# First two weight tiles of a three-block layer kernel worked by pairs of row blocks

## The chip, the cores and the metric

One core of one Trainium2 chip runs the whole program. The metric is the device time of one execution in microseconds (us); lower is better. Times inside an execution are us from the start of its span.

## The reference, cut to what matters

Three blocks run one after the other on x of 512 rows and 2048 columns, all in float32. The part that the change touches is the head of block 1:

```
h = x * rsqrt(mean(x*x, axis=-1) + 1e-6) * norm_pre      # rows of x, 512 x 2048
proj = h @ w_in                                          # 2048 x 5120 weights
u_s, g_s, q_d, k_d, v_d, g_d, q_x, g_x = split(proj)     # u_s: the first 1024 columns
```

u_s goes into a state-space scan, the others into two kinds of attention and gates; a memory of 256 rows is normalised and projected too. The mixed result is multiplied by w_out, normalised and added to x. Blocks 2 and 3 have the same outline (norm, projection, mixing, output projection) with other mixers.

## The kernel before, in words

**Precision.** A float32 product is made of three passes over rounded parts: a value is split into an upper part (`hi`, rounded to fp32r) and a lower part (`lo`, the rest). For a weight slice and the activations h the kernel adds hi x hi, hi x lo(h) and lo x hi(h).

**Weights.** A weight tile is 128 columns wide and 2048 deep. It comes in two slices of 128 x 1024 (8 steps k of 128 each) through a ring of four slots. SP issues the loads in order (L3198); the load of a slot's next slice waits until TensorE has used the old one: `part_used` for the first slice of a tile, the bank's full semaphore for the last. ScalarE makes the upper part (L3350, `split`), VectorE the lower (L3392).

**Head of block 1.** Rows are taken in four blocks of 128 (`tt` 0 to 3). For each: `x_rstd` makes the sum of squares (blocks 0 and 3 on ScalarE, L723; blocks 1 and 2 on VectorE, L885), the mean (VectorE, L887), the root (ScalarE, L725), the reciprocal and a diagonal matrix of it (VectorE, L889, L891). `x_turn` multiplies the rows by that diagonal on TensorE (L506), which turns and scales them at once: four quarters of a PSUM bank, eight matmul records each. `x_parts` takes the bank into the upper part of h on ScalarE (L745, sixteen instructions, four a bank) and the lower part on VectorE (L911, sixteen), which then frees the bank. The lower part overlies the rows of x in SBUF.

**Banks.** `x_turn` and the small transposes `ss_0` (L529, for the state matrix) take their banks in turn from the five side banks 3 to 7, and each take waits until the bank's former user is released (`bk.take`). Tiles take theirs from banks 0 to 2.

**Tiles.** A tile in mode "T" keeps the weights stationary and moves the 512 rows: 16 steps k, three passes each, 48 matmuls of 512 columns into one bank (L3265). Tile 0 (`ut[0]`) waits at every fourth k for the release of all four row blocks' quarter (`first_tile_waits`). Then ScalarE copies the bank to `us` (L694) and GpSimd stores it (L430).

**Order.** One list, `script`, sets the order of the work on every engine: each engine walks it and does its own share of each step. In it stand, for the head, x_rstd 0, x_turn 0, x_rstd 1, x_turn 1, x_parts 0, x_rstd 2, x_turn 2, x_rstd 3, x_turn 3, b1_tables (GpSimd loads, after the fourth turn), x_parts 1 to 3, ss_0, then tile 0, ss_1, tile 1, ss_2, the norms of the memory (m_rstd), tile 2, m_turn 0, ss_3, tile 3, m_turn 1, powers, tile 4. The split steps are put in by a loop (L3087 on): a slice's step goes in ahead of a `target` step. In the kernel before, tile 0's first slice is split ahead of x_parts 3, and its second and both of tile 1 ahead of tile 0, behind ss_0. Tile 2's are split ahead of tile 1, that is behind ScalarE's copy of tile 0.

The matmuls of block 2 at L3275 are of another mode ("N"): h is stationary and a weight slice 256 columns wide moves. They are named here since the prediction reads their rows.

Of the kernel before, what the change touches and what calls it, by code (L numbers as in the profile page):

```python
# [13 lines left out]
P = 128  # L14
# [3 lines left out]
TT = SEQ // P  # L18
# [4 lines left out]
SLOT = 1024  # L23
# [107 lines left out]
def block1(K):  # L131
    nc, T, ps, bk = K.nc, K.T, K.ps, K.bk
# [49 lines left out]
    t = K.arena(0, Bf)  # L182
# [5 lines left out]
    t = K.arena(0, Bf)  # L188
# [8 lines left out]
    w = K.arena(vst_at)  # L197
# [4 lines left out]
    w = K.arena(rope_at)  # L202
    ang, kk_ = w("ang", SEQ), w("turns", SEQ)
    w = K.arena(rope_at)
    scan_1, scan_2 = w("scan_1", 2, 8, S_G // 2), w("scan_2", 2, 8, S_G // 2)
    w = K.arena()
# [7 lines left out]
    w = K.arena()  # L214
# [12 lines left out]
    def tile(name, i):  # L227
# [7 lines left out]
        else:  # L235
# [1 line left out]
        return st  # L237


    script = [("x_rstd", 0), ("x_turn", 0), ("x_rstd", 1), ("x_turn", 1), ("x_parts", 0), ("x_rstd", 2), ("x_turn", 2),  # L240
              ("x_rstd", 3), ("x_turn", 3), ("b1_tables", 0), ("x_parts", 1), ("x_parts", 2), ("x_parts", 3), ("ss_0", 0)]
    ut = [tile("us", i) for i in range(S_C)]
    mt = [t_ for h in range(XA_H) for t_ in (tile("mk", h), tile("mv", h))]
# [5 lines left out]
    glu = [tile("glu", i) for i in range(8)]  # L249
# [41 lines left out]
    n = 0  # L291
# [225 lines left out]
        pe.wait_ge(s_diag, TT + tt + 1)  # L517
        turn_rows(pe, st, mem_rows[:, tt, :], diag[:, tt, :])

    def first_tile_waits(pe, kk):  # L520
        if kk % 4 == 0:
            for tt in range(TT):
                pe.wait_ge(*bk.released(("x_turn", tt), kk // 4))

    def pe_ss_0(pe, st):
# [752 lines left out]

    def glu_waits(pe, kk):
        pe.wait_ge(s_clo, kk + 1)  # L1280
    K.tiles[ut[0]]["by_k"], K.tiles[glu[0]]["by_k"] = first_tile_waits, glu_waits
    K.stage("pool", b1_tables=pool_tables, tile1=pool_tile, sp_a=pool_sp_a, sp_b=pool_sp_b,
            scan=pool_scan, sp_d=pool_sp_d, y_back=pool_y_back, wo1=pool_wo)
    K.stage("pe", x_turn=pe_x_turn, m_turn=pe_m_turn, ss_0=pe_ss_0, sp_a=pe_sp_a, sp_b=pe_sp_b, sp_c=pe_sp_c, sp_d=pe_sp_d,
# [1579 lines left out]
class Kit:  # L2864


    def __init__(self, nc, ctx, T):
        self.nc, self.ctx, self.T = nc, ctx, T
        self.at = {"pe": {}, "act": {}, "vec": {}, "pool": {}}
        self.uses, self.tiles, self.params = {}, {}, {}  # L2870
        self.norm_gain, self.par_count, self.wo_src = {}, {}, {}
        self.y_base, self.y_count = {}, 0
        self.slot_src, self.slot_count, self.slot_used = {}, {"wo": 8}, {}
        self.const_loads, self.wait_gain, self.par_at = [], {}, 0
        self.sp_start, self.mix_parts, self.norm_parts, self.norm_gain_wait = [], {}, {}, {}
        self.sq_junk, self.wo_releases = {}, {}
        self.wo_mids, self.mids, self.wo_order, self.mix_wait, self.mix_src = {}, {}, {}, {}, {}

    def keep(self, *dims):
# [34 lines left out]
    def tile(self, st, srcs, mode, w, act, n, kt=KT, bias=None, after=(), releases=1, lo=None,  # L2914
             lo_from=0, full=None):


        self.tiles[st] = dict(srcs=srcs, mode=mode, w=w, act=act, n=n, kt=kt, bias=bias, after=list(after),
                              releases=releases, lo=lo, per=SLOT // max(w, P), lo_from=lo_from, full=full, pool="P", by_k=None)

    def rounded(self, name, *dims):

# [9 lines left out]
def build(nc, T, out, blocks):  # L2932
    with ExitStack() as ctx:
        K = Kit(nc, ctx, T)
# [10 lines left out]
        ring, ring_lo = K.rounded("ring", RING, SLOT)  # L2945
        ring_hi = K.sb("ring_hi", RING, SLOT, dt=F32R)
# [13 lines left out]
        full = [K.sem(f"bank{i}_full") for i in range(8)]  # L2960
# [3 lines left out]
        part_used = K.sem("part_of_stage_used")  # L2964
        s_hi, s_lo = K.sem("weight_upper_ready"), K.sem("weight_lower_ready")
# [70 lines left out]
        script = []  # L3036
# [10 lines left out]
        for blk in blocks:  # L3047
# [3 lines left out]
            if blk in K.norm_parts:  # L3051
                for tt in range(TT):
                    after = script.index(("norm", blk, min(tt + 1, TT - 1)))
# [17 lines left out]
        def slot_subs(st):  # L3071
            return K.tiles[st]["kt"] // K.tiles[st]["per"] if st[0] == "tile" else K.slot_count.get(st[0], 0)
# [10 lines left out]
        for n, st in enumerate(script):  # L3083
            subs = slot_subs(st)
            for sub in range(subs):
                slots.append((st, sub))
                stage_at[st] = n  # L3087
                if is_split(st, sub):
                    target = st if sub >= 2 or len(slots) == 2 else earlier if subs == 1 else before
                    assert len(slots) <= RING or stage_at[slots[-1 - RING][0]] <= stage_at[target]  # L3090
                    ahead.setdefault(target, []).append(("split", st, sub))
            if subs:
                before, earlier = st, before
# [14 lines left out]
        script = [s_ for st in script for s_ in order(st)]  # L3108
        split_no = {st[1:]: n for n, st in enumerate([st for st in script if st[0] == "split"])}

        for st in script:
# [3 lines left out]
            elif st[0] == "tile":  # L3115
                t = K.tiles[st]
# [12 lines left out]
        slot_of, slot_value, slot_view, count, loads = {}, {}, {}, [0] * RING, []  # L3129
        parts = 0  # L3130
        for n, (st, sub) in enumerate(slots):
            i = n % RING
            if st[0] == "tile":
                t = K.tiles[st]
# [8 lines left out]
                subs = slot_subs(st)  # L3143
            elif st[0] in K.slot_src:
                view = lambda r, i=i: r[:, i, :]
                dmas = K.slot_src[st[0]](st, sub, ring[:, i, :])
                last, subs = K.slot_used[st[0]](st, sub), 1
            else:
                w = K.wo_src[st[1]][0]
# [3 lines left out]
                last, subs = bk.filled(st, 3), 8  # L3153
# [21 lines left out]
        def columns(ap, kk, tt=None):  # L3175
# [4 lines left out]
                return ap[:, :, kk, :] if tt is None else ap[:, tt, kk, :]  # L3180
            return ap[:, kk, :] if tt is None else ap[:, kk, tt * P:(tt + 1) * P]

        block = ctx.enter_context(nc.Block())

        @block.sync
# [33 lines left out]
        def _(pe):  # L3219
            pe.wait_ge(K.s_const, const_total)  # L3220
            pe.wait_ge(s_made, 2)
            for st in script:
                if st in inner:
                    continue
                if st[0] == "norm":
                    pe.wait_ge(s_hn, hn_at[st] + 1)
                    for k4 in range(KT // 4):
                        bk.take(pe, st, k4)
# [220 lines left out]
```

## Time and profile before

| | |
|---|---|
| median of 3 runs | 3064.72 us |
| lowest, highest | 3061.41, 3065.34 us |
| profiled execution | 3060.2 us |
| its span | 3058.4 us |
| TensorE matmul busy | 2925.0 us, 96% |
| VectorE, ScalarE, GpSimd busy | 46%, 35%, 10% |
| mean granted clock of TensorE | 0.969 |

The profiled execution is one run of its own; its span is from the first to the last instruction, and its own time has 1.8 us around that. In the rows further down PE is TensorE, PEld its weight loads, DVE VectorE, ACT ScalarE, POOL GpSimd and SPq the queue of SP, which issues DMAs. Busy shares are means over the whole program and tell nothing of a single stage.

### The profile page before, as it was taken

The page shows a single profiled execution, that of the slowest core. Times are in us where ns is not written, and L with a number is a line of the kernel's source. Part 1 is how long each engine was busy: PE and PEld are TensorE (multiplying, and loading weights), DVE is VectorE, ACT ScalarE, POOL GpSimd, SP SyncE. Part 2 cuts the span into 40 slices and gives each one's busy share as a digit, 9 for nine tenths or more (in the row PEclk, how much of TensorE's full clock was granted, in tenths as well). Part 3 has the DMA queues.
Part 4 walks back from the last instruction along what each step waited for, and adds up shares of the span by engine and source line. Part 5 has one row for each costly group of instructions (what it writes and reads, how often), then busy time and mean ns, then how long its engine had stood idle before and what let it go on. Part 6 is the DMA issues. An engine that isn't in the chain of part 4 may idle for free.

```text
span 3058.4 us, 36911 instructions
## 1 busy us (share of the span) xinstructions
PE 2925.0 (96%) x14916; PEld 2366.6 (77%) x14916; DVE 1414.3 (46%) x2435; ACT 1057.2 (35%) x1740; POOL 302.3 (10%) x530
## 2 busy tenths in 40 slices
PE   7999999999988999999999977999999999999997
PEld 6788878888866888888887865777777776777786
DVE  5566634445234545545544234135444543443533
ACT  5223233453235333222223245235444542222321
POOL 5346044100000000000000000000000000000000
PEclk9999999999998999999999988999999999999999
DMA  7466455324334544465664332332222222222332
GB/s 187 113 173 126 105 118 124 101 83 166 97 109 131 151 145 131 145 186 173 189 181 159 97 116 62 82 91 69 72 67 70 69 76 69 62 62 76 128 98 105
DMA packets 440136, 349.05 MB, mean 114 GB/s; under 512 B 72352, under 2 KB 389984, under 8 KB 435744
## 3 DMA queue, kind: packets, MB, share of 16 engines
q1 hardware_dynamic: 406544, 241.86, 28.6%
q0 software_dynamic: 33424, 104.84, 11.9%
q8 instruction: 119, 1.95, 0.3%
q14 instruction: 49, 0.40, 0.0%
HBM read 322.78 MB, written 22.81 MB: 113 GB/s over the span
## 4 chain that ended last, share of the span: by engine, by line
PE 91%; DVE 4%; ACT 3%; issue 1%; DMA 0%; DVEq 0%; SPq 0%; ACTq 0%
PE bank L3265 56%; PE bank L3301 17%; PE bank L3275 3%; PE bank L2183 1%; PE bank L2234 1%; PE bank L2210 1%; PE bank L2255 1%; PE bank L589 1%; PE bank L584 1%; PE bank L2294 1%; PE bank L653 1%; PE bank L2152 1%; PE bank L506 1%; PE bank L2312 1%; PE bank L554 0%
## 5 line engine op out<-in xcount | busy, mean ns | idle before, releaser
L3392 DVE TENSOR_TENSOR ring_parts<-ring,ring_hi 128x1024 fp32r<-128x1024 f32 (+1 forms) x420 | 505.5, 1217 | 805.9 <-ACT ring_hi L3350 801.7
L3265 PE MATMUL bank<-A_parts,ring_hi 128*128 128x512 f32 (+1 forms) x1616 | 655.5, 406 | 24.8 <-DVE ring_parts L3392 17.8
L3350 ACT ACTIVATE ring_hi<-ring 128x1024 fp32r<-128x1024 f32 (+1 forms) x420 | 437.2, 1053 | 658.6 <-DMA ring<-in_w_in 347.3
L3265 PE MATMUL bank<-A_parts,ring_parts 128*128 128x512 f32 (+1 forms) x1616 | 637.1, 394 | 0.0
L3265 PE MATMUL bank<-X_parts,ring_hi 128*128 128x512 f32 (+1 forms) x1424 | 557.6, 392 | 0.0
L3265 PE MATMUL bank<-B_parts,ring_hi 128*128 128x512 f32 (+1 forms) x1272 | 503.9, 396 | 4.5 <-DVE X_parts L3380 4.5
L3265 PEld LDWEIGHTS bank<-A_parts,ring_hi 128*128 128x128 f32 (+1 forms) x1616 | 307.3, 190 | 100.6 <-issue 30.2
L3265 PEld LDWEIGHTS bank<-A_parts,ring_parts 128*128 128x128 f32 (+1 forms) x1616 | 306.7, 190 | 70.9 <-issue 0.6
L3265 PEld LDWEIGHTS bank<-X_parts,ring_hi 128*128 128x128 f32 (+1 forms) x1424 | 267.8, 188 | 57.3 <-issue 2.0
L3265 PE MATMUL bank<-B_parts,ring_parts 128*128 128x512 f32 (+1 forms) x784 | 305.8, 390 | 0.0
L3301 PE MATMUL bank<-ring_hi,A_parts 128*128 128x512 f32 x768 | 301.1, 392 | 1.6 <-issue 0.9
L3301 PE MATMUL bank<-ring_hi,B_parts 128*128 128x512 f32 x768 | 300.7, 392 | 1.8 <-DVE A_parts L3399 1.8
L3265 PEld LDWEIGHTS bank<-B_parts,ring_hi 128*128 128x128 f32 (+1 forms) x1272 | 239.9, 189 | 61.1 <-issue 6.3
L3265 PE MATMUL bank<-work_parts,ring_hi 128*128 128x512 f32 (+1 forms) x616 | 231.1, 392 | 0.0
L3301 PE MATMUL bank<-ring_parts,A_parts 128*128 128x512 f32 x512 | 199.9, 390 | 0.0
L3301 PEld LDWEIGHTS bank<-ring_hi,A_parts 128*128 128x128 f32 x768 | 145.3, 189 | 33.3 <-issue 3.1
L3265 PEld LDWEIGHTS bank<-B_parts,ring_parts 128*128 128x128 f32 (+1 forms) x784 | 145.8, 186 | 32.6 <-issue 0.7
L3301 PEld LDWEIGHTS bank<-ring_hi,B_parts 128*128 128x128 f32 x768 | 145.3, 189 | 32.3 <-issue 1.8
L3265 PEld LDWEIGHTS bank<-work_parts,ring_hi 128*128 128x128 f32 (+1 forms) x616 | 115.0, 187 | 24.5
L1764 DVE SCALAR_TENSOR_TENSOR work<-work,par 128x1024 f32<-128x1024 f32 x90 | 115.5, 1283 | 3.0
L2438 ACT ACTIVATE work<-work 128x128 f32<-128x128 f32 (+3 forms) x128 | 70.5, 553 | 132.3 <-DVE work L2598 132.3
L1744 POOL DMA_DIRECT2D work<-in_w_ada x96 | 50.7, 528 | 639.6 <-DVE work L1764 519.6
(507 smaller groups left out, 3322.6 us busy)
## 6 DMA issues: line engine op xcount, KB each, us to landing
ring<-in_w_in SPq DMA_DIRECT2D x288, 512.0 KB, 3.8
ring<-in_w_out SPq DMA_DIRECT2D x96, 512.0 KB, 3.7
work<-in_w_ada POOLq DMA_DIRECT2D x96, 512.0 KB, 4.7
ring<-in_w_in SPq DMA_DIRECT2D x48, 256.0 KB, 3.7
ring<-in_w_mem_kv SPq DMA_DIRECT2D x16, 512.0 KB, 4.2
x_keep<-X POOLq DMA_DIRECT2D x8, 1024.0 KB, 4.7
X<-x_keep POOLq DMA_DIRECT2D x8, 1024.0 KB, 10.2
X<-in_x SPq DMA_DIRECT2D x4, 1024.0 KB, 10.6
```

The source lines that it names most:

```text
L506: mm = nc.tensor.matmul(ps(st, k4)[:, j * P:(j + 1) * P], lhsT=rows[:, kk * P:(kk + 1) * P], rhs=scale, start=True, stop=True)
L584: nc.tensor.matmul(cols[r], lhsT=T2[c % 2][:, g * P:(g + 1) * P], rhs=U2[c % 2][:, g * S_B:(g + 1) * S_B], start=True, stop=False)
L589: mm = nc.tensor.matmul(cols[r][:, 1:S_B], lhsT=C2[c % 2][rows, s, q, :], rhs=vst[rows, s, 0:S_B - 1, 4 * c + q], start=False, stop=(s == 1))
L653: mm = nc.tensor.matmul(ps(st)[:, 0:P], lhsT=pT[:, u % 2, kt * P:(kt + 1) * P], rhs=rhs, start=(kt == 0), stop=(kt == n - 1))
L1744: pool.dma_start(slots[:, n % ADA_SLOTS, :], T["w_ada_3"][0][kp * P:(kp + 1) * P, part * ADA_W:(part + 1) * ADA_W]).then_inc(s_load[n % AD ...
L1764: ins = nc.vector.scalar_tensor_tensor(acc[:, :], w, sc[:, kp:kp + 1], acc[:, :], ALU.mult, ALU.add)
L2438: nc.scalar.activation(e, e, ACT.Exp, bias=mx[:, n % 2, i:i + 1], scale=-1.0, accum_out=sums[:, n % 2, i:i + 1]).then_inc(s_exp, 1)
L3265: mm = nc.tensor.matmul(K.ps(st)[0:w, 0:t["n"]], lhsT=wp[:, j, :], rhs=columns(ap, kk), start=first, stop=end)
L3275: mm = nc.tensor.matmul(o, lhsT=columns(ap, kk, tt), rhs=wp[:, j, :], start=first and opens and t["bias"] is None, stop=end, skip_group_ch ...
L3301: mm = nc.tensor.matmul(K.ps(st, tt), lhsT=y[:, kk, rows], rhs=w[:, j, :], start=(no == 0 and m == 0), stop=(no == KT - 1 and m == 2), ski ...
L3350: nc.scalar.activation(slot_view[key](ring_hi), slot_view[key](ring), ACT.Copy).then_inc(s_hi, 1)
L3392: nc.vector.tensor_tensor(slot_view[key](ring_lo), slot_view[key](ring), slot_view[key](ring_hi), ALU.subtract).then_inc(s_lo, 1)
```

## The change

The change does three things. The sum of squares of row block 2 (`x_rstd` 2) moves ahead of `x_parts` 0 in the script. The four split steps of tiles 0 and 1 all move ahead of `x_parts` 2. And TensorE works tiles 0 and 1 together in two passes (`tiles_by_pair`): for row blocks 0 and 1 both tiles with all their k, then for row blocks 2 and 3 both tiles again, out of the same slices, which stay in the ring. Each matmul then moves 256 columns. The waits for the parts of h are for the pair's two row blocks alone. A slot is given back in the second pass.

```diff
-    script = [("x_rstd", 0), ("x_turn", 0), ("x_rstd", 1), ("x_turn", 1), ("x_parts", 0), ("x_rstd", 2), ("x_turn", 2),
+    script = [("x_rstd", 0), ("x_turn", 0), ("x_rstd", 1), ("x_turn", 1), ("x_rstd", 2), ("x_parts", 0), ("x_turn", 2),
               ("x_rstd", 3), ("x_turn", 3), ("b1_tables", 0), ("x_parts", 1), ("x_parts", 2), ("x_parts", 3), ("ss_0", 0)]
...
-    def first_tile_waits(pe, kk):
+    def first_tile_waits(pe, kk, pair):
         if kk % 4 == 0:
-            for tt in range(TT):
+            for tt in (2 * pair, 2 * pair + 1):
                 pe.wait_ge(*bk.released(("x_turn", tt), kk // 4))
...
-    K.tiles[ut[0]]["by_k"], K.tiles[glu[0]]["by_k"] = first_tile_waits, glu_waits
+    K.tiles[ut[0]]["by_pair"], K.tiles[glu[0]]["by_k"] = first_tile_waits, glu_waits
+    K.paired_tiles[1] = ut[0:2]
+    for st in ut[0:2]:
+        for sub in range(2):
+            K.split_at[st, sub] = ("x_parts", 2)
...
                     target = st if sub >= 2 or len(slots) == 2 else earlier if subs == 1 else before
+                    target = K.split_at.get((st, sub), target)
...
+        def row_pair(ap, kk, pair):
+
+            if isinstance(ap, tuple):
+                ap, kk = ap[kk // 8], kk % 8
+            if len(ap.shape) == 4:
+                return ap[:, 2 * pair:2 * pair + 2, kk, :]
+            return ap[:, kk, 2 * pair * P:2 * (pair + 1) * P]
...
+            def tiles_by_pair(sts):
+
+                for pair in range(2):
+                    for st in sts:
+                        t = K.tiles[st]
...
+                        if pair == 0:
+                            bk.take(pe, st)
+                        subs, w, per = slot_subs(st), t["w"], t["per"]
+                        o = K.ps(st)[0:w, 2 * pair * P:2 * (pair + 1) * P]
+                        for sub in range(subs):
+                            pe.wait_ge(s_lo, split_no[st, sub] + 1)
+                            hi, lo = slot_view[st, sub](ring_hi), slot_view[st, sub](ring_lo)
+                            for j in range(per):
+                                kk = sub * per + j
+                                if t["by_pair"]:
+                                    t["by_pair"](pe, kk, pair)
+                                for n, (wp, ap) in enumerate(((hi, t["act"]), (hi, t["lo"]), (lo, t["act"]))):
+                                    mm = nc.tensor.matmul(o, lhsT=wp[:, j, :], rhs=row_pair(ap, kk, pair),
+                                                          start=pair == 0 and kk == 0 and n == 0,
+                                                          stop=pair == 1 and kk == t["kt"] - 1 and n == 2, skip_group_check=True)
+                            if pair == 1 and sub < subs - 1:
+                                mm.then_inc(part_used, 1)
+                        if pair == 1:
+                            mm.then_inc(bk.full_sem(st, 0), 1)
+
             for st in script:
                 if st in inner:
                     continue
-                if st[0] == "norm":
+                if st in in_pairs:
+                    if st in [sts[0] for sts in K.paired_tiles.values()]:
+                        tiles_by_pair(K.paired_tiles[st[1]])
+                elif st[0] == "norm":
```

## Rows read from the trace of the kernel before

**Rows 1.** The page: the chain that ended last, by line, share of the span.

```profile
PE bank L3265 56%; PE bank L3301 17%; PE bank L3275 3%; PE bank L2183 1%; PE bank L2234 1%; PE bank L2210 1%; PE bank L2255 1%; PE bank L589 1%; PE bank L584 1%; PE bank L2294 1%; PE bank L653 1%; PE bank L2152 1%; PE bank L506 1%; PE bank L2312 1%; PE bank L554 0%
```

**Rows 2.** The chain within the first 60 us: start, length, piece.

```profile
27.47 5.50 PE bank L506 x24
...
35.30 1.13 DVE ring_parts L3392
36.43 1.05 DVE X_parts L911 x4
...
37.61 22.51 PE bank L3265 x98
```

**Rows 3.** Timeline of VectorE, 0 to 60: start, length, instruction, count, [idle before].

```profile
14.65 0.29 DVE L891 TENSOR_SCALAR work<-ident,rstd 128x128 f32<-128x128 f32 x1
...
20.20 2.28 DVE L885 CUSTOM_DVE_ANT_0 work<-X 128x2048 f32<-128x2048 f32 x1
...
26.29 7.33 DVE L911 SCALAR_TENSOR_TENSOR X_parts<-bank,par,A_parts 128x128 fp32r<-128x128 f32 x28 [0.55 <-ACT A_parts L745]
...
41.77 3.50 DVE L3392 TENSOR_TENSOR ring_parts<-ring,ring_hi 128x1024 fp32r<-128x1024 f32 x3 [1.21 <-ACT ring_hi L3350]
```

**Rows 4.** Waits of TensorE, 60 to 300: us in total, times, longest.

```profile
PE bank L3265 <- DVE ring_parts L3392: 4.0, 1, 4.0
```

**Rows 5.** The chain behind the second turn of memory rows.

```profile
88.63 0.69 DVE B L921
...
103.49 23.66 PE bank L3265 x96
```

**Rows 6.** The loads of x (L3190): issues, and time to landing.

```profile
L3190 SPq DMA_DIRECT2D X<-in_x x4: 416/428/655, 1.2 to 2.6; - x4
...
DMA to landing us min/median/max: 5.2/10.6/16.7
```

**Rows 7.** Timeline of ScalarE, 0 to 60.

```profile
14.33 1.13 ACT L745 ACTIVATE A_parts<-bank,par 128x128 fp32r<-128x128 f32 x4
...
22.82 1.89 ACT L723 ACTIVATE work<-X 128x2048 f32<-128x2048 f32 x1
...
25.13 7.34 ACT L745 ACTIVATE A_parts<-bank,par 128x128 fp32r<-128x128 f32 x28
...
40.70 2.94 ACT L3350 ACTIVATE ring_hi<-ring 128x1024 fp32r<-128x1024 f32 x3
```

**Rows 8.** Timeline of SP's queue, 0 to 60: loads of slices, then of memory rows.

```profile
3.30 18.85 SPq L3198 DMA_DIRECT2D ring<-in_w_in  x4
22.19 2.48 SPq L375 DMA_DIRECT2D B<-in_mem  x2
```

**Rows 9.** Stretches: busy and count of PE, PEld, DVE, ACT, POOL; clock, DMA, GB/s.

```profile
21.30:26.00 4.70, 1.16 (x8) 0.97 (x8) 2.39 (x8) 3.07 (x8) 0.00 (x0) 1.00 1.19 295
26.00:33.00 7.00, 5.53 (x26) 5.53 (x27) 6.71 (x26) 6.47 (x26) 0.00 (x0) 0.51 0.87 331
33.00:36.60 3.60, 3.60 (x33) 3.48 (x33) 3.06 (x9) 3.60 (x12) 0.00 (x0) 1.00 0.00 0
```

**Rows 10.** Timeline of TensorE: the small transposes ahead of tile 0.

```profile
36.50 0.33 PE L529 MATMUL bank<-ident,work 64*128 64x64 f32 x2
```

**Rows 11.** Two pieces of the whole chain; weight loads in the stretch of the second.

```profile
221.58 10.93 PE bank L3265 x48
...
980.98 22.81 PE bank L3275 x190
...
L3275 PEld LDWEIGHTS bank<-ring_hi,X_parts 128*128 128x128 f32 x64 | 8.8, 192 | 0.0
```

**Rows 12.** The slice loads (L3198) issued from 40 to 56.

```profile
DMA to landing us min/median/max: 3.9/4.2/4.7
```

**Rows 13.** Timeline of GpSimd, 35 to 60: its stores of tile 0.

```profile
51.99 4.25 POOL L430 DMA_DIRECT2D u_blocks<-work  x8
```

**Rows 14.** The core's span and mean granted clock.

```profile
core 0: 3058.4 us, clock 0.969
```

More of the change, by code:

```diff
@@ L2876, in __init__ @@
         self.sq_junk, self.wo_releases = {}, {}
+        self.split_at, self.paired_tiles = {}, {}
         self.wo_mids, self.mids, self.wo_order, self.mix_wait, self.mix_src = {}, {}, {}, {}, {}
@@ L2918, in tile @@
         self.tiles[st] = dict(srcs=srcs, mode=mode, w=w, act=act, n=n, kt=kt, bias=bias, after=list(after),
-                              releases=releases, lo=lo, per=SLOT // max(w, P), lo_from=lo_from, full=full, pool="P", by_k=None)
+                              releases=releases, lo=lo, per=SLOT // max(w, P), lo_from=lo_from, full=full, pool="P", by_k=None, by_pair=None)
     def rounded(self, name, *dims):
@@ L3221, in _ @@
             pe.wait_ge(s_made, 2)
+            in_pairs = {st for sts in K.paired_tiles.values() for st in sts}
+            def tiles_by_pair(sts):
+                for pair in range(2):
+                    for st in sts:
+                        t = K.tiles[st]
+                        assert t["mode"] == "T" and t["bias"] is None and st not in K.mids and not t.get("wait")
+                        for dep in t["after"]:
+                            if dep[0][2] // 2 == pair:
+                                pe.wait_ge(*bk.released(*dep))
+                        if pair == 0:
[17 more added lines that the diff above has]
+                            mm.then_inc(bk.full_sem(st, 0), 1)
             for st in script:
```

## The prediction, made before the changed kernel was run

> **What bounds the kernel now.** I read the chain of waits first: every line of any size in it is TensorE's, and the first, the split matmuls of the weight tiles (L3265), holds 56% [rows 1]. The kernel as a whole is bound by TensorE, so a change pays only if it takes TensorE's waits away or shortens its work. The change touches the first 60 us, so next I read the same chain there. It starts the weight tiles at 37.61 and from there runs 22.51 us through 98 matmuls with no other piece: tiles 0 and 1 are worked without a hole [rows 2]. Ahead of 37.61 the chain lies on VectorE and ScalarE: they make the parts of h out of the turned rows. VectorE ends row block 2 at 35.3, makes one weight slice (35.30, 1.13 of it on the chain), and ends the first quarter of row block 3 at 37.5, which releases TensorE [rows 2, 3]. So the first tile waits only for a quarter of row block 3, not for all of it: the change has little to win there.
>
> What follows the first tiles matters too. From 59.5 TensorE goes on through turns and tiles until a wait of 4.0 us before 103.49, and what it then waits for (the powers of the state matrix on VectorE) starts only when TensorE has ended its second turn of memory rows, at 88.6 [rows 4, 5]. A time won or lost by 59.5 is therefore carried on one for one; that wait absorbs nothing.
>
> **Squares of row block 2 forward.** VectorE is free at 14.94 and takes the square (2.28 us) there instead of at 20.20 [rows 3]. The four issues of x land 5.2 to 16.7 us after issue, median 10.6, the last issued at 2.6 [rows 6]; spread evenly, block 2 is there at about 14.6 (an estimate), so no wait. But the step moves on ScalarE as well: its root stands now ahead of row block 0's parts, which started at 14.33 [rows 7] and now start only behind the root. From the square's start (20.20) to ScalarE's first work behind the root (22.82) it was 2.6 us; so 14.94 + 2.6 = 17.6, 3.3 us later. ScalarE makes a part in 7.34/28 = 0.262 us, VectorE in 7.33/28 = 0.262, a block of 16 in 4.2 [rows 3, 7]. ScalarE ends block 0 at 21.8, squares block 3 and takes its root (22.82 to 25.13, 2.3 us): block 1's parts start at 24.1 on ScalarE, and 1.15 later, at 25.3, on VectorE, where they started at 26.29. **Gain 1.0 us.** VectorE ends block 1 at 29.5. TensorE's second turn is later than before (its banks are released from 19.9 on, where it was 16.6), but it ends at 22.9 and ScalarE wants it from 24.1: free.
>
> **The four slices forward.** The split steps of both slices of both tiles now stand ahead of row block 2's parts, on ScalarE and on VectorE. Before, one slice stood ahead of block 3 and three behind it, hidden beside tile 0. One costs 1.06 us on ScalarE (three in 2.94) and 3.50/3 = 1.17 on VectorE [rows 3, 7]. VectorE: 29.5 + 4.7 = 34.15. The four slices were issued by 22.15 with 2.1 MB of memory rows behind them [rows 8]; from 26 to 33, when the queue runs dry, 7 x 331 GB/s = 2.3 MB were moved [rows 9], so the last slice was in by about 27.5 and nothing is waited for. Block 2's parts then run on VectorE from 34.15 to 38.35; before they ended at 35.3. **Loss 3.05 us**, the gain above already in it.
>
> **TensorE cannot start before that.** It takes its work in order: the fourth turn, the small transposes ss_0 (L529), then tile 0. The side banks go round by five. The fourth turn's quarters 1, 2 and 3 take the banks of block 2's quarters 0, 1 and 2, and ss_0 takes that of quarter 3. So ss_0 waits for the end of block 2's parts whatever the tile waits for, and the row pair 0 can start only behind it: 38.4 + 0.3 = 38.7. The tile's wait for row block 3 is gone, but it was worth only the stretch from 36.83 (the end of ss_0) to 37.61, 0.8 us [rows 2, 10].
>
> **The clock in this stretch.** TensorE's granted clock was 0.51 over 26 to 33, after it had worked 1.16 us in the 4.7 before; 24 turn matmuls took 5.50 us there (0.229 each) and 33 fell in 3.60 us at a granted 1.00, the full 2.4 GHz (0.109) [rows 2, 9]. In the new order TensorE has done the fourth turn's first quarter by 31.6 to 33.3, then has nothing until the first quarter of block 2 is released at 35.35: the same picture as at 24.5 to 27.5. I expect the clock to fall to 1.2 GHz once more at about 36.3. The last two quarters (8 records each) then take 1.7 us each instead of 0.9, and end at 39.8 instead of 38.3: tile 0 starts at 40.15. Bounds: no fall, 38.7; a fall that lasts 7 us, as the one seen, and reaches into the tiles, 3.5 us of half matmuls at half speed, 1.75 lost on top, 41.9. I take 40.15, since the seen fall came after just such a gap.
>
> **Half-width matmuls.** 96 matmuls of 512 columns become 192 of 256, each with its own weight load. The nearest rows are the 256-column matmuls of block 2 (L3275), same types, a load for each: 22.81 us for 190, 0.120 each; the 512-column ones take 10.93/48 = 0.2277 [rows 11]. So 192 x 0.120 = 23.04 against 96 x 0.2277 = 21.86: **loss 1.2 us**. The loads of 190 ns in the records are beside the matmuls there, as 0.120 is less than one of them. The lower bound for the term is zero (256 columns at half of 0.2277), the upper one that each load shows in full (a rival below). The Trainium skill ("TensorE: Matmul & The Clock Gate", section "Back-to-back issue gap") gives N/2.4 + 2.5 ns for matmuls back to back, 109 ns for 256 and 216 for 512; by it the split into halves would cost 0.24 us. The rows differ from it in both sizes, 120 and 228 ns, and the sum goes by the rows.
>
> **Behind it.** Row pair 0 of both tiles takes 11.5 us, to 51.7; block 3's parts are done on VectorE by about 42.2, so pair 1 waits for nothing. The ring is the other thing: tile 0's first slot was free 24 matmuls in, at 43.1, now only after pair 1 has used it, 51.7 + 2.9 = 54.6. Landing took 3.9 to 4.7 us in this stretch [rows 12], the split 1.06 + 1.2 more: tile 2's first slice is ready at 61.2, wanted at 63.2. Hidden with 2 us to spare, where it was about 8. If that cover went, each us of a later landing over 2 would be a us of the end. GpSimd's tables start with the fourth turn's end, 3.2 us later, and end at 55.2 instead of 51.99; tile 0's stores, queued behind, now wait for its bank at 58 anyway [rows 13]. They are needed far later. On the DMA queue of the weights (SP) nothing else changes place. ss_1 on VectorE comes earlier, and nobody waits for it.
>
> **Sum.** Tile 2 starts at 40.15 + 23.05 = 63.2, where it was 59.5: +2.55 for the start (37.6), +1.15 for the halves, **+3.7 us**. The profiled execution took 3060.2 us around a span of 3058.4, so it would be 3063.9; it lies 4.5 us under the median of the three runs, 3064.72, to which I add the 3.7: 3068.4. That is 0.12%, and a measurement of this kernel can tell about 0.2% (6.1 us) from nothing.
>
> **Rivals.**
> (1) The clock does not fall: start at 38.7, +2.2 us, 3066.9. For it: the gap is short, and work stands on both sides. Against: the fall seen at 26. Chance 0.28.
> (2) The fall is long or late and reaches into the tiles: up to +5.5, 3070.2. The start of the seen fall lay 1.7 us behind the end of the work before; a little later here is enough. Chance 0.12.
> (3) Slower outright, by the weight loads: if a load of 190 ns [rows 11] is not beside a matmul of 256 columns in this direction (weights stationary, rows moving), each pair takes 0.19: 192 x 0.19 = 36.5 against 21.9, and with the later start +17 us, 3082. It decides from 0.132 us a matmul, where the loss passes 6.1. Against it stands 0.120 in L3275. Chance 0.04. The same page's section "LDWEIGHTS" gives the load as P/1.2, 107 ns for 128 columns, about one such matmul, where the records show 192: by the page the load would just be covered.
> (4) Faster: the intended effect, in which tile 0 starts when row blocks 0 and 1 are ready. It would need the fourth turn and ss_0 out of its way; the order of TensorE and the banks speak against it. At 30.7, behind the first quarter of the fourth turn, it would give 7 less 1.2, some -5.8 us, 3058.9. What else could bring that: the mean granted clock is 0.969 [rows 14], so 2 x 0.031 x 3058 = 190 us are granted at 1.2 GHz, and a shift of the work against the falls of the clock could take 10 or 20 of them away, each worth half. Chance 0.04.
> (5) Tile 2's first slice late by a landing of 8 us or more: +2 and more on top. Nothing in the rows shows one here. Chance 0.04, its other cases in the range.
> The forecast has 0.48. Together with the scatter of the runs (3061.41 to 3065.34) this gives faster 0.04, same 0.84, slower 0.12. The range, from the lowest run + 2.2 to the highest + 5.5 and a little: 3063.5 to 3072. Most of the chance is on a loss too small to be told.
>
> **What the profile after will show.** First L3265 record near 40 (38.7 without the fall); VectorE ending block 2's parts at 38.3 with four splits just ahead; the granted clock at 0.5 in 36 to 40; 192 matmuls of 256 columns in 23.0 us; tile 2 from 63.2 with no wait for ring_parts; the 4.0 us wait before the powers still there, near 103 to 107. I am wrong if tile 0 starts before 37.6, if a half matmul takes over 0.13 us, or if a wait for the ring stands before tile 2.

## The result, and the profile after

The changed kernel takes 3069.03 us in the median of 14 runs (3063.6 to 3073.14), the kernel before, run beside it, 3062.74 (14 runs, 3060.22 to 3065.34). The ratio is 1.0021, with a 95% interval of 1.0012 to 1.0029: 6.3 us slower, between 3.7 and 8.9, and a second set of runs further down gives 1.0013. Forecast were +3.7 us and a range of 3063.5 to 3072. The profiled execution took 3064.93 us around a span of 3063.1; against the one of before, 3060.2 around 3058.4, that is +4.7. The chain of the whole kernel is the old one, with tiles 0 and 1 on a line of their own (L3259), L3265 now L3313 and L3275 now L3323, as against [rows 1]:

```profile
PE bank L3313 54%; PE bank L3349 17%; PE bank L3323 3%; PE bank L2187 1%; PE bank L2238 1%; PE bank L2214 1%; PE bank L2259 1%; PE bank L3259 1%; PE bank L589 1%; PE bank L584 1%; PE bank L2156 1%; PE bank L2298 1%; PE bank L653 1%; PE bank L2316 1%; PE bank L554 0%
```

The chain within the first 70 us, start, length and piece, where [rows 2] stood before (L745 and L911 make the parts, L723 and L885 the squares, L3440 the lower parts of slices):

```profile
17.66 4.23 ACT A_parts L745 x16
21.88 1.90 ACT work L723 x2
...
25.26 4.23 DVE X_parts L911 x16
29.49 4.54 DVE ring_parts L3440 x4
34.03 1.04 DVE X_parts L911 x4
...
35.12 5.49 PE bank L506 x24
40.60 0.40 PE bank L529 x2
41.01 23.26 PE bank L3259 x192
64.27 5.92 PE bank L3313 x26
```

Read it from the top. The square of row block 2 is taken right behind that of block 1, row block 0's parts start on ScalarE only at 17.66 (before: 14.33 [rows 7]), and block 1's start on VectorE at 25.26 instead of 26.29 [rows 3]. Then the four slices stand in VectorE's way for 4.54 us. The first quarter of block 2's parts frees a bank at 35.1, and from there the chain is the fourth turn and ss_0, not the tile: the tile starts at 41.01, where it was 37.61, and does not wait for parts of h at all. Its 192 half matmuls, those of tiles 0 and 1, take 23.26 us. Tile 2 starts at 64.27. Before, ScalarE copied tile 1's bank at 59.71, and now at 64.30, 0.03 us behind the start of tile 2; in the second trace further down it is 0.04. So tile 2 started at about 59.67 before, and is 4.6 us later (ScalarE's timelines, before and after):

```profile
59.71 0.60 ACT L694 ACTIVATE work<-bank 128x512 f32<-128x512 f32 x1 [5.06 <-PE bank L3265]
...
64.30 0.60 ACT L694 ACTIVATE work<-bank 128x512 f32<-128x512 f32 x1 [0.67 <-PE bank L3259]
```

The stretches of that execution (busy and count of PE, PEld, DVE, ACT, POOL; granted clock, DMA share, GB/s), as [rows 9]:

```profile
34.20:41.00 6.80, 5.88 (x27) 5.54 (x27) 6.80 (x28) 5.67 (x22) 0.33 (x1) 0.50 0.00 0
41.00:64.20 23.20, 23.20 (x194) 23.20 (x194) 5.77 (x22) 5.04 (x9) 19.27 (x34) 1.00 0.65 136
```

The fall of the clock is there, 0.50 from 34.2 to 41.0, and 1.00 over the two tiles. It covers all three remaining quarters: 24 records in 5.49 us, 0.229 each, the half-speed figure of [rows 2]. The same trace has an earlier fall, from about 27.4 to 30.7, on the third turn's quarters; it is not on the chain.

A third of the weight loads of the 256-column matmuls between 41 and 64.1 (count, busy, mean ns, idle before), 192 ns a load as in [rows 11]:

```profile
L3259 PEld LDWEIGHTS bank<-A_parts,ring_hi 128*128 128x128 f32 x64 | 12.3, 192 | 0.1
```

And TensorE's waits within the first 110 us (total, times, longest):

```profile
PE bank L506 <- DVE X_parts L911: 6.0, 3, 3.1
PE bank L3313 <- DVE ring_parts L3440: 4.0, 1, 4.0
```

There is no wait for the ring or for row blocks 2 and 3 inside tiles 0 and 1 or ahead of tile 2. The 4.0 us wait before the powers stands as it stood [rows 4]: it took up nothing, as it ended at 103.49 before [rows 5] and ends at 108.12 now, 4.6 us later like tile 2. ScalarE's and VectorE's share for tile 2's first slice (ScalarE's timeline, then VectorE's):

```profile
59.99 1.06 ACT L3398 ACTIVATE ring_hi<-ring 128x1024 fp32r<-128x1024 f32 x1 [0.85 <-DMA ring<-in_w_in]
...
61.08 1.23 DVE L3440 TENSOR_TENSOR ring_parts<-ring,ring_hi 128x1024 fp32r<-128x1024 f32 x1 [14.98 <-ACT ring_hi L3398]
```

The slice is ready at 62.3 and used at 64.3: the cover that the prediction put at 2 us measured 2.0.

### The profile page after: what moved, and what is told of

Same layout as the page of the kernel before. It is cut to its first block, busy times and chain, and to the rows that moved or that the text cites. A ratio compares the mean times of both kernels' runs of the same rounds, so it can differ in the third digit from the quotient of the medians.

```text
span 3063.1 us, 37103 instructions
## 1 busy us (share of the span) xinstructions
PE 2930.2 (96%) x15012; PEld 2375.5 (78%) x15012; DVE 1414.1 (46%) x2435; ACT 1057.1 (35%) x1740; POOL 301.9 (10%) x530
## 4 chain that ended last, share of the span: by engine, by line
PE 90%; DVE 5%; ACT 3%; issue 1%; DMA 1%; DVEq 0%; SPq 0%; ACTq 0%
PE bank L3313 54%; PE bank L3349 17%; PE bank L3323 3%; PE bank L2187 1%; PE bank L2238 1%; PE bank L2214 1%; PE bank L2259 1%; PE bank L3259 1%; PE bank L589 1%; PE bank L584 1%; PE bank L2156 1%; PE bank L2298 1%; PE bank L653 1%; PE bank L2316 1%; PE bank L554 0%
## 5 line engine op out<-in xcount | busy, mean ns | idle before, releaser
L3440 DVE TENSOR_TENSOR ring_parts<-ring,ring_hi 128x1024 fp32r<-128x1024 f32 (+1 forms) x420 | 505.4, 1217 | 815.0 <-ACT ring_hi L3398 810.9
L3313 PE MATMUL bank<-A_parts,ring_hi 128*128 128x512 f32 x1584 | 642.6, 406 | 24.1 <-DVE ring_parts L3440 17.9
L3313 PE MATMUL bank<-A_parts,ring_parts 128*128 128x512 f32 x1584 | 624.5, 394 | 0.0
L3313 PE MATMUL bank<-X_parts,ring_hi 128*128 128x512 f32 (+1 forms) x1392 | 545.3, 392 | 0.0
L3313 PE MATMUL bank<-B_parts,ring_hi 128*128 128x512 f32 (+1 forms) x1272 | 503.7, 396 | 4.5 <-DVE X_parts L3428 4.5
L3313 PEld LDWEIGHTS bank<-A_parts,ring_hi 128*128 128x128 f32 x1584 | 301.0, 190 | 98.7 <-issue 29.6
L3313 PEld LDWEIGHTS bank<-A_parts,ring_parts 128*128 128x128 f32 x1584 | 300.5, 190 | 69.6 <-issue 0.4
L3313 PE MATMUL bank<-B_parts,ring_parts 128*128 128x512 f32 (+1 forms) x784 | 306.0, 390 | 0.0
L3313 PEld LDWEIGHTS bank<-X_parts,ring_hi 128*128 128x128 f32 (+1 forms) x1392 | 261.9, 188 | 55.9 <-issue 2.3
L3313 PEld LDWEIGHTS bank<-B_parts,ring_hi 128*128 128x128 f32 (+1 forms) x1272 | 239.9, 189 | 61.2 <-issue 6.6
L3313 PE MATMUL bank<-work_parts,ring_hi 128*128 128x512 f32 (+1 forms) x616 | 231.2, 392 | 0.0
L3313 PEld LDWEIGHTS bank<-B_parts,ring_parts 128*128 128x128 f32 (+1 forms) x784 | 145.8, 186 | 32.8 <-issue 0.8
L3313 PEld LDWEIGHTS bank<-work_parts,ring_hi 128*128 128x128 f32 (+1 forms) x616 | 115.0, 187 | 24.5
```

Source lines behind the costliest of these rows:

```text
L3313: mm = nc.tensor.matmul(K.ps(st)[0:w, 0:t["n"]], lhsT=wp[:, j, :], rhs=columns(ap, kk), start=first, stop=end)
L3440: nc.vector.tensor_tensor(slot_view[key](ring_lo), slot_view[key](ring), slot_view[key](ring_hi), ALU.subtract).then_inc(s_lo, 1)
```

## The experiments

For each kernel the start of tile 2, where its trace shows it on the chain or by ScalarE's copy of tile 1's bank (L694), says what the head of the program costs; the time says it too, with some us of scatter that come from elsewhere.

**The changed kernel again.** No edit.

> The changed kernel once more, for a second trace. Theory (the start of tile 0 is set by VectorE's order and by a fall of TensorE's clock in the last turn, whose place differs from run to run): tile 0 starts between 38.6 (no fall) and 42, the end of row block 2's parts on VectorE stays at 38.2 within 0.3 us, and 192 half matmuls take 23.0 to 23.3 us where no low clock reaches them. Rival (the halves or the ring cost more in the runs that take longer): a wait for ring_parts ahead of tile 2, or more than 0.125 us for a half matmul at a granted 1.00. Time 4 to 7 us over the kernel before.

3065.38 us in the median of 12 runs (3063.59 to 3072.62), ratio 1.0013 (1.0004 to 1.0021). The chain, then the stretch of the fall:

```profile
34.94 4.59 PE bank L506 x24
39.53 0.27 PE bank L529 x2
39.79 23.22 PE bank L3259 x192
63.02 7.05 PE bank L3313 x31
```

```profile
35.70:39.20 3.50, 3.50 (x19) 3.50 (x18) 3.50 (x15) 3.50 (x14) 0.00 (x0) 0.51 0.00 0
```

VectorE releases the bank within 0.2 us of the other execution (34.94 against 35.12), but the clock falls at 35.7 instead of 34.2 and for half as long: the same 24 records take 4.59 us instead of 5.49, and tile 2 starts 1.25 earlier, +3.35 on before (59.67). The halves are unmoved, 23.22 us. This execution is near the one that the prediction drew (40.15, 63.2, +3.7). So the theory holds, and the rival's wait for the ring does not appear in either trace.

**Full width.** Tiles 0 and 1 in 512 columns, one after the other; splits and square as changed.

```diff
-            for tt in (2 * pair, 2 * pair + 1):
+            for tt in range(TT):
...
-    K.tiles[ut[0]]["by_pair"], K.tiles[glu[0]]["by_k"] = first_tile_waits, glu_waits
-    K.paired_tiles[1] = ut[0:2]
+    K.tiles[ut[0]]["by_k"], K.tiles[glu[0]]["by_k"] = first_tile_waits, glu_waits
```

> The changed kernel with tiles 0 and 1 worked one after the other in 512 columns again; the square and the four splits stay where the change put them. Theory: tile 0 starts at the same place as in the changed kernel (38.6 to 41, behind ss_0, no wait for row block 3), the two tiles take 21.9 us instead of 23.1, so 1.2 us less than the changed kernel and 3.4 to 5 more than the kernel before. Rival (halves are free, all of the loss is the later start): same time as the changed kernel. Rival (the pairs bring their start forward): tile 0 starts later here than in the changed kernel.

3065.51 us (11 runs), ratio 1.0007 (0.9998 to 1.0015). Its chain (all tiles are on L3312 here):

```profile
34.96 4.43 PE bank L506 x24
39.39 0.40 PE bank L529 x2
39.79 30.43 PE bank L3312 x133
```

Tile 0 starts at 39.79, just where the paired kernel beside it started, and also waits for no parts: the waits that the pairs take away were not binding in this order. ScalarE copies tile 1 at 61.87 here and at 63.06 in the second trace with pairs: the pairs cost 1.2 us and bring nothing.

```profile
61.87 0.60 ACT L694 ACTIVATE work<-bank 128x512 f32<-128x512 f32 x1 [3.65 <-PE bank L3312]
...
63.06 0.60 ACT L694 ACTIVATE work<-bank 128x512 f32<-128x512 f32 x1 [0.52 <-PE bank L3259]
```

The times of the two cannot be told apart (1.0013 and 1.0007, intervals overlap), the traces can.

**The square alone.** The kernel before with the square of row block 2 forward, nothing else.

```diff
-... ("x_turn", 1), ("x_parts", 0), ("x_rstd", 2), ("x_turn", 2),
+... ("x_turn", 1), ("x_rstd", 2), ("x_parts", 0), ("x_turn", 2),
```

> The kernel before with nothing but the sum of squares of row block 2 moved ahead of row block 0's parts. Theory: VectorE begins block 1's parts 1.0 us earlier (25.3), tile 0 starts at about 36.4 instead of 37.6, and the kernel is 1 to 1.5 us faster than before, within what can be told or just under it. Rival (ScalarE's 3.3 us later start on block 0 is not made good): no gain or a loss of up to 3 us.

3059.44 us (11 runs) beside 3062.15, ratio 0.9990 (0.9981 to 1.0000).

```profile
25.11 8.36 DVE X_parts L911 x32
33.47 1.13 DVE ring_parts L3392
...
35.78 32.95 PE bank L3265 x144
```

VectorE goes through blocks 1 and 2 without the pause that it had before. Tile 0 starts 1.8 us earlier (35.78 against 37.61), and tile 1 is copied at 57.89, also 1.8 us earlier. The expectation was 1.2: it left out the 0.5 us that VectorE waited inside block 2's parts before (the hole between the end of the 28 parts of [rows 3] at 33.62 and 34.17), for a quarter turned at low clock. The rival (ScalarE's late start is not made good) falls in this trace. Run once more, the same kernel gave less.

> The kernel before with the square alone forward, once more, to set it beside the reordered passes on the same chip. Theory: tile 0 starts at 35.8 and tile 2 at 57.7, 1.8 us under the kernel before, ratio 0.9990 to 0.9995. Rival (the gain of the first measurement was chance): ratio of 1.000 or over.

3059.69 us beside 3060.80, ratio 0.9998 (0.9989 to 1.0007), inside the forecast of 0.9990 to 0.9995 only by its interval. The tiles on the chain of this execution, and in it the stretch of the fall:

```profile
35.94 34.39 PE bank L3265 x144
```

```profile
35.70:39.10 3.40, 3.16 (x8) 2.51 (x9) 3.20 (x13) 3.37 (x11) 3.40 (x6) 0.50 0.50 116
```

The start is the same within 0.2 us, but the clock was at 0.50 for the tile's first 3.4 us, and 144 matmuls took 34.39 us instead of 32.95. Tile 1 is copied at 59.49, only 0.2 us before the 59.71 of the kernel before. The kernel before has a fall too, over 26 to 33 [rows 9]; here it came later, at the end of TensorE's 1.9 us wait for the tile's parts, and on the tile itself, where it cost 1.4 us.

**The gap filled.** The changed kernel with 14 products of the identity between the first and second quarter of the fourth turn.

```diff
     def turn_rows(pe, st, rows, scale):
         for k4 in range(KT // 4):
+            if st == ("x_turn", 3) and k4 == 1:
+                for n in range(14):
+                    nc.tensor.matmul(ps(ut[2])[:, 0:P], lhsT=K.ident[:, :], rhs=K.ident[:, :], start=True, stop=True)
```

> The changed kernel with 14 products of the identity with itself (28 records of 128 columns, about 3.1 us at full clock, into a bank that tile 2 overwrites, read by nobody) put in TensorE's idle stretch between the first and the second quarter of the fourth turn. Theory (fall of the clock): the granted clock stays at 1.00 from 31 to 41, the last three quarters take 0.9 us each and end 1.1 behind the releases, tile 0 starts at 38.6 to 38.9 and tile 2 at 62 instead of 64.1: 2.4 us less than the changed kernel in a run with a fall, some 2 us in the median, and a narrower spread. Rival (the gap costs nothing beyond the wait for VectorE): the same time as the changed kernel, or up to 0.5 us more if the filling delays the second quarter.

3064.95 us (11 runs), ratio 1.0008 (0.9999 to 1.0016). The stretch of the last turn, granted 0.50 in the changed kernel's first trace, and the chain (the turn is L509 here, ss_0 L532, the pair L3262):

```profile
34.20:41.00 6.80, 6.06 (x48) 5.73 (x49) 6.80 (x27) 6.78 (x25) 2.77 (x4) 1.00 0.06 19
```

```profile
34.94 3.23 PE bank L509 x24
38.17 0.27 PE bank L532 x2
38.44 23.23 PE bank L3262 x192
61.67 8.41 PE bank L3316 x37
```

With TensorE kept at work ahead of it the clock stays at 1.00, the three quarters run at VectorE's pace (3.23 us for 24 records, 5.49 with the fall), and tile 0 starts at 38.44, near the 38.7 of rival (1); tile 2 starts at 61.67, +2.0 where that rival had +2.2. The price of the fall in the first trace is thus 5.49 + 0.40 less 3.23 + 0.27, 2.4 us, in the second 1.35. In all four traces with this gap unfilled (the changed kernel twice, full width, the square back) the clock fell in or behind it, at 34.2, 35.7, 36.4 and 36.3, and 24 records took 4.43 to 5.49 us; in this one, with the same turn and releases at the same times, it did not. What the fall costs is read from these chains. That the filling prevents it rests on one trace, and falls come at places that differ from run to run, so that is evidence and no proof. In the time the gain could not be told from the run beside it, and the spread is hardly narrower (8.6 us against 9.0), where a clear effect was expected.

**The square back.** The changed kernel with the square where it was.

> The changed kernel with the sum of squares of row block 2 back behind row block 0's parts. Theory: VectorE begins block 1's parts at 26.2 to 26.3 instead of 25.1 to 25.3 and ends block 2's at 39.2; tile 0 starts at 39.7 (no fall of the clock) to 42.3, and the kernel is 1.0 us slower than the changed one, 5 to 7 over the kernel before. Rival (the square's place does not matter here, as the splits stand between): same as the changed kernel.

3067.35 us (10 runs) beside 3062.64, ratio 1.0017 (1.0008 to 1.0026).

```profile
25.97 4.23 DVE X_parts L911 x16
...
35.83 4.57 PE bank L506 x24
40.40 0.27 PE bank L529 x2
40.66 23.23 PE bank L3259 x192
```

The release of the first bank of block 2, at 35.8, is 0.7 to 0.9 us later than in the two changed traces, a little less than the 1.0 expected; the fall costs 1.35 here as well, by 4.57 + 0.27 against the 3.23 + 0.27 of the filled gap. The times do not separate it from the changed kernel.

**The splits back.** The changed kernel without `split_at`: one slice ahead of block 3's parts, three behind.

```diff
     K.paired_tiles[1] = ut[0:2]
-    for st in ut[0:2]:
-        for sub in range(2):
-            K.split_at[st, sub] = ("x_parts", 2)
```

> The changed kernel with the four splits where the kernel before had them: one ahead of row block 3's parts, three behind them; pairs and square as changed. Theory (order of VectorE): block 2's parts end at 33.5 instead of 38.2, TensorE is past the fourth turn and ss_0 at 34.8 and starts tile 0 at about 34.8, when its first slice is made; 24 half matmuls on, at 37.7, it waits for the second slice, which VectorE makes only behind block 3's parts, ready at about 40.2 to 41; so a new wait of 2.5 to 3 us inside tile 0, and tile 2 at about 60.7 to 61.2: 1.2 to 1.7 over the kernel before, some 3 under the changed kernel. Rival (the loss comes from the halves and the pair order, not from the splits): no better than the changed kernel.

3067.66 us (10 runs), ratio 1.0016 (1.0007 to 1.0025). Its chain and TensorE's wait (the pair is L3256 here):

```profile
37.44 1.28 ACT L751
...
39.97 1.24 DVE ring_parts L3437
...
41.25 21.91 PE bank L3256 x168
63.16 10.91 PE bank L3310 x48
```

```profile
PE bank L3256 <- DVE ring_parts L3437: 4.2, 2, 3.4
```

The wait came as foretold, but at 3.4 us instead of 2.5 to 3: ScalarE's table load for ss_0 (1.28) stands ahead of the second slice. And the idle time let the clock fall on the tile behind it: 0.50 over 41.9 to 45.3 in this trace, and 168 half matmuls took 21.91 us where 0.121 each make 20.3: 1.6 us. Tile 2 starts at 63.16 instead of 60.7 to 61.2. So the splits forward were needed for the pairs; left back, they cost as much in the other place (63.16 with this fall, 63.02 and 64.27 in the changed kernel with its own). The expected saving of 3 us is a miss.

**Passes first.** Splits of tile 0 ahead of block 2's parts, of tile 1 ahead of block 3's, and TensorE's order changed:

```diff
...
+                if st == ("x_turn", 3):
+                    t0, t1 = K.paired_tiles[1]
+                    pe.wait_ge(K.s_diag, 4)
+                    K.last_turn(pe, range(1))
+                    tiles_by_pair(None, [(0, t0)])
+                    K.last_turn(pe, range(1, 4))
+                    tiles_by_pair(None, [(0, t1)])
+                    K.at["pe"]["ss_0"](pe, ("ss_0", 0))
+                    tiles_by_pair(None, [(1, t0), (1, t1)])
```

> TensorE's order changed so that the first pass needs nothing of row blocks 2 and 3: first quarter of the fourth turn, row pair 0 of tile 0, the other three quarters, row pair 0 of tile 1, ss_0, row pair 1 of both; tile 0's slices are split ahead of block 2's parts, tile 1's ahead of block 3's; square forward as changed. Theory: tile 0 starts at 30.7 to 31.3 behind its first slice, the quarters run at 36.6 to 39.3, tile 1's pair 0 to 45.1, pair 1 of both to 56.9 to 57.5 with no wait; tile 2 about 2.4 us before its place in the kernel before (59.5) and 7 before that in the changed one: 3059 to 3060 against 3062. Rival (the waits only move: pair 1 or the ring of tile 2 becomes late): a wait for X_parts or ring_parts of over 1 us, and no gain over the kernel before.

3059.71 us (11 runs) beside 3062.64, ratio 0.9995 (0.9985 to 1.0004). A gain over the kernel before cannot be told. From the first release on its chain is TensorE's alone (the pair is L3264 here, tile 2 L3328):

```profile
26.27 5.61 PE bank L506 x32
31.88 5.75 PE bank L3264 x48
37.63 2.68 PE bank L506 x24
40.31 5.75 PE bank L3264 x48
...
46.32 11.70 PE bank L3264 x96
58.02 10.91 PE bank L3328 x48
```

Here the pairs do what they can do: tile 0 starts at 31.88, 9 us before the changed kernel, and nothing waits up to tile 2. Tile 2 at 58.02 is 6.25 us earlier than in the changed kernel's first trace, 5.0 than in its second, and 1.65 earlier than before; 2.4 were expected. The first piece shows why: 32 turn records took 5.61 us, where 4.33 do without a fall, as the clock had fallen again behind the gap at 24 to 26. The square alone, without pairs, reached the same place: tile 1 copied at 57.89, tile 2 from 57.85.

**Passes first, gap filled.** The run before with nine products of the identity ahead of the third turn's second quarter.

```diff
+            if st == ("x_turn", 2) and k4 == 1:
+                for n in range(9):
+                    nc.tensor.matmul(ps(ut[2])[:, 0:P], lhsT=K.ident[:, :], rhs=K.ident[:, :], start=True, stop=True)
```

> The order of the run before (pass over row blocks 0 and 1 first) with 9 products of the identity (18 records, 2.0 us at full clock, read by nobody) in TensorE's idle stretch between the first and second quarter of the third turn, 24.1 to 26.2. Theory (the fall of the clock behind that gap held up the quarters ahead of tile 0): no fall before 60, the next four quarters end at 29.8 to 30.3, tile 0 starts behind its first slice at 30.7 instead of 31.9 and tile 2 at 56.8 instead of 58.0; 3058.5 to 3059.5 against 3062.5 for the kernel before. Rival: the fall comes all the same or the first slice is the later of the two; same as without the filling.

3060.13 us (11 runs) beside 3060.80, ratio 1.0001 (0.9992 to 1.0010). The clock held in the traced execution (stretch behind the filling, granted 0.69 in the run before), but that is no evidence for the filling: of the eight traces with the square forward and this gap of 2.1 us unfilled, four show a fall behind it (the changed kernel's first, full width, the square alone once, passes first) and four none. The chain shows the next thing in line (the pair is L3267 here, tile 2 L3331):

```profile
26.00:31.00 5.00, 4.90 (x38) 4.35 (x37) 5.00 (x16) 5.00 (x16) 0.00 (x0) 1.00 1.03 398
```

```profile
48.42 6.55 DMA ring<-in_w_in
...
54.99 1.07 ACT ring_hi L3416
...
56.08 1.24 DVE ring_parts L3458
...
57.36 11.18 PE bank L3331 x48
```

A landing of 6.55 us used up the cover of the ring and made tile 2 wait 0.4 us; it starts at 57.36 instead of 56.8. It is no single late one: the slices loaded in this stretch landed 5.7 to 6.9 us after issue here and 5.5 to 6.8 in the run before, against 4.0 to 4.9 in the changed kernel's two traces. Why they are slower in this order is open. That is 2.3 us earlier than before, of which 2.0 are left where the wait before the powers ends (101.49 against 103.49), and no gain can be told in the time.

## Why the prediction was right, and which term was short

- **What bounds the head.** Right. The first tile waited for little before (0.8 us), and the chain ahead of it is mostly VectorE's order. Full width in the new order starts at the same 39.79: the pairs free TensorE of nothing there.
- **The square forward, gain 1.0.** Right in its working: 17.66 for 17.6 on ScalarE, 25.26 and 25.08 for 25.3 on VectorE. Only the end of TensorE's second turn was read too early, 24.3 for 22.9, and that cost nothing: ScalarE did not wait for it. In the changed kernel the square is worth 0.7 to 0.9 us (the square back). By itself, in the kernel before, it was worth 1.8 us in the head in one trace and 0.2 in the other, where a fall took the rest.
- **The four slices.** Right: 4.54 us against 4.7, release of the first bank at 35.1 and 34.9 for 35.35. This is the main loss: block 2's parts end at 38.1 on VectorE where they ended at 35.3, 2.8 us with the square's gain in it, where 3.05 was forecast.
- **TensorE cannot start before ss_0.** Right, and shown from the other side: with the passes put ahead of the turn's last quarters the same tile starts at 31.88 instead of 41.01.
- **The clock.** The mechanism was right, and its size is the term that differs from run to run. The prediction let the fall begin at about 36.3 and reach two quarters, tile 0 at 40.15. In the first trace it began at 34.2 and took all three and ss_0, tile 0 at 41.01; in the second it began at 35.7, tile 0 at 39.79. The gap filled gives 38.44. The term is 2.4 us in the first trace and 1.35 in the second, where 1.45 was forecast (40.15 less 38.7); full width and the square back, with falls at 36.4 and 36.3, also give 1.35. So three of four traces have the size that was forecast, and the one taken with the result does not.
- **Half-width matmuls, 1.2.** Right: 23.26, 23.22, 23.23 us for 192 in three traces, 0.121 each, against 23.04 forecast; 1.2 us by the copies of tile 1. Rival (3), a load that shows, falls. The Trainium skill ("TensorE: Matmul & The Clock Gate", section "Back-to-back issue gap") gives N/2.4 + 2.5 ns, 109 for 256 columns and 216 for 512, but calls that the gap of an isolated matmul; for a stream of weight loads and matmuls it gives about 131 ns at 512 columns and no figure for 256. The runs show 121 and, at 512, 228 [rows 11], so neither of its figures fits here; the difference between two halves and one whole is 14 ns here and 2.5 by the formula, so by it the pairs would have looked almost free.
- **Behind it.** Right: a loss in the head is carried on, tile 2 at +4.6 and +3.35 in the two traces, the end of the wait before the powers at +4.6 and +3.3, and their spans at +4.7 and +3.5. In full width, the square alone and the gap filled the end of that wait also moved with the head, by +2.2, -1.8 and +2.0. That the two spans agree so well is in part luck: the gap filled had +2.0 in the head and +9.2 in the span. The ring was covered by 2.0 us, as worked out; landings of 5.5 to 6.9 us, as in the two kernels with the passes first, would have used that up.
- **The time.** The heads carry +3.35 and +4.6, the medians +6.3 and +3.2 with intervals of 3.7 to 8.9 and 1.2 to 6.4. Together they speak for a loss of about 4. The absolute figure was nearer than the difference by luck: 3068.4 was forecast from a base of 3064.72, the median of three runs, and 3069.03 measured, while the base turned out at 3062.74, so 2.0 us too much in the base hid most of the 2.6 missing in the difference. The scatter goes with the clock: in the 14 runs a mean granted clock of 0.969 stands beside 3063.6 and 3064.9 us, one of 0.965 or 0.966 beside 3072.3 to 3073.1. A straight line through each set of runs, read at a clock of 0.968, gives 3066.9 and 3067.2 for the changed kernel's two sets and 3063.1 for the 35 runs of the kernel before beside the second, so some +4 (an estimate: the clocks are given to 0.001, which goes with 2 us). Where in the program the first set was at the low clock more often is open: no trace was taken of the runs at 3072 to 3073. The rest does move by itself. The full-width execution had a span of 3068.8 us at a mean granted clock of 0.965, the kernel before 3058.4 at 0.969, while their heads differ by 2.2 us. Its clock alone is 2 x 0.004 x 3060, an estimate of some 24 us more at low and up to 12 us of work lost, which can hold the other 8.
- **Chances.** 0.84 stood on a loss or gain under 0.2%; the measured 0.21% lies on that border, and its interval on both sides of it.

## What to carry to other kernels

Splitting the work so that it can start on half of its input pays only where that input is what it waits for. Here TensorE's own order (a turn, a small transpose, and the banks they reuse) stood between, and moving that order, with tile 1's two slices put one block later, brought tile 2 forward by 6.25 or 5.0 us against the changed kernel's two traces, where the split alone lost 1.2. Even so it got no farther than the square alone did without any pairs (58.02 and 57.85). Before making work startable earlier, follow the engine's queue and the resources of the steps ahead of it; then look at what was moved forward to feed it (here four slices, 4.54 us on the engine that was the bottleneck of the head).

Among the versions tried, the square alone, one pair of entries swapped, measured lowest beside its own runs of before (0.9990 and 0.9998). Run beside the changed kernel it beats it clearly (0.9981 to 1.0000 against 1.0004 to 1.0021), and the kernel before not clearly.

## What the runs showed of the hardware

- The granted clock fell in or behind idle gaps of TensorE of 1.9 to 4.4 us, and not behind each: the gap of 2.1 us at 24 to 26 had a fall in four traces of eight. In the last turn it fell at 34.2 in one execution and 35.7 in another of the same kernel, at 0.50 for 6.8 and 3.5 us. Same work, 24 turn records: 5.49, 4.59, and 3.23 us without a fall. With products that nobody reads in the gap it did not fall: in one trace against four with a fall for the gap ahead of 35, and in one against four with and four without for the gap at 24 to 26, so the second shows nothing.
- What a fall costs depends on what it lands on: 2.4 us on the last turn of the changed kernel, 1.4 us on the first tile in the kernel with the square alone (144 matmuls in 34.39 instead of 32.95 us), 1.6 us on the tile in the kernel with the splits back (168 half matmuls in 21.91 us instead of 20.3).
- Matmuls of 256 columns with a weight load each run at 0.121 us, of 512 at 0.228, with loads recorded at 192 and 188 ns each and, inside tiles 0 and 1, next to no idle time: at 256 columns a load's record is longer than the 121 ns a matmul takes, so the loads stay beside the matmuls.
